# Turning attention weights by two rounded products with a unit matrix, at the head of each double step, instead of by plain fp32 transposes

## The reference

```
s = einsum('bqhd,bkhd->bhqk', q_i, k) * scale     # plus bias or decay, masked
p = softmax(s, axis=-1)
out = einsum('bhqk,bkhd->bqhd', p, v)
```

## Time and profile before

| | us |
|---|---|
| median of 3 runs (1578.36 to 1581.55) | 1580.87 |
| the profiled execution's own time | 1582.88 |
| its span, first to last instruction | 1581.0 |
| PE busy in it | 1538.2 (97%) |
| DVE busy | 1005.7 (64%) |
| ACT busy | 712.1 (45%) |
| POOL busy | 563.0 (36%) |

### The profile page before, as it was taken

How to read it: one execution, slowest core, us unless ns; L and a number is a source line. 1 busy time by engine, 2 the same in 40 slices (tenths; PEclk the granted TensorE clock), 3 DMA queues, 4 the chain that set the end, 5 groups by cost and what they waited for, 6 DMA issues and landing times.

```text
span 1581.0 us, 35399 instructions
## 1 busy us (share of the span) xinstructions
PE 1538.2 (97%) x15704; PEld 1414.6 (89%) x15704; DVE 1005.7 (64%) x1637; ACT 712.1 (45%) x1126; POOL 563.0 (36%) x452
## 2 busy tenths in 40 slices
PE   9999999999999999999999999999999999999998
PEld 8989987899978989987999989999998899999887
DVE  4364386878784445576777786766446777764356
ACT  4554534544445455435444444633332555433223
POOL 3745613000217745503000310734673006446640
PEclk9999999999999999999999999999999999999999
DMA  9433364787545423474676545453333354533332
GB/s 357 169 122 108 113 232 191 265 299 273 187 166 211 161 89 125 161 279 187 250 283 240 204 142 182 152 176 133 135 136 135 124 197 153 182 133 138 114 130 93
DMA packets 43944, 281.49 MB, mean 178 GB/s; under 512 B 5144, under 2 KB 5272, under 8 KB 14352
## 3 DMA queue, kind: packets, MB, share of 16 engines
q1 hardware_dynamic: 42192, 270.13, 47.4%
q0 software_dynamic: 1600, 9.10, 1.5%
HBM read 278.15 MB, written 1.06 MB: 177 GB/s over the span
## 4 chain that ended last, share of the span: by engine, by line
PE 78%; DVE 13%; ACT 3%; issue 3%; POOL 2%; DMA 0%; POOLq 0%; SPq 0%; ACTq 0%; DVEq 0%
PE ps L613 75%; DVE part0l L1453 3%; DVE part1l L1453 3%; PE ps L621 3%; ACT part0h L2523 1%; DVE rows L1890 1%; ACT part1h L2523 1%; DVE Pr L1887 1%; ACT gates L2520 1%; ACT Xh L2523 1%; DVE Xl L1468 1%; DVE small L1484 0%; DMA ring<-in_w 0%; DVE raw L2012 0%; DVE mgx L2144 0%
## 5 line engine op out<-in xcount | busy, mean ns | idle before, releaser
L2523 ACT ACTIVATE part1h<-ring 128x1024 fp32r<-128x1024 f32 (+1 forms) x216 | 215.8, 1047 | 226.0 <-PE ps L613 213.6
L2523 ACT ACTIVATE part0h<-ring 128x1024 fp32r<-128x1024 f32 (+1 forms) x216 | 213.0, 1035 | 209.6 <-PE ps L613 194.3
L613 PE MATMUL ps<-Xh,part1h 128*128 128x256 f32 x968 | 276.7, 286 | 7.5 <-DVE Xl L1468 2.4
L613 PE MATMUL ps<-Xh,part0h 128*128 128x256 f32 (+1 forms) x952 | 270.9, 285 | 3.4 <-DVE Xl L1468 1.3
L613 PE MATMUL ps<-Xl,part1h 128*128 128x256 f32 x968 | 271.1, 280 | 0.0
L613 PE MATMUL ps<-Xh,part1l 128*128 128x256 f32 x968 | 270.9, 280 | 0.0
L613 PE MATMUL ps<-Xl,part0h 128*128 128x256 f32 (+1 forms) x952 | 265.2, 279 | 0.0
L613 PE MATMUL ps<-Xh,part0l 128*128 128x256 f32 (+1 forms) x952 | 265.1, 278 | 0.0
L3020 POOL TENSOR_TENSOR part1l<-ring,part1h 128x512 fp32r<-128x512 f32 x144 | 185.3, 1317 | 102.5 <-ACT part1h L2523 102.3
L3020 POOL TENSOR_TENSOR part0l<-ring,part0h 128x512 fp32r<-128x512 f32 x144 | 185.3, 1318 | 101.8 <-ACT part0h L2523 101.7
L1453 DVE TENSOR_TENSOR part1l<-ring,part1h 128x1024 fp32r<-128x1024 f32 (+1 forms) x144 | 181.3, 1299 | 52.3 <-ACT part1h L2523 52.0
(11 more groups left out here) (446 smaller groups left out, 3260.4 us busy)
## 6 DMA issues: line engine op xcount, KB each, us to landing
ring<-in_w SPq DMA_DIRECT2D x211, 1024.0 KB, 4.9
hid<-in_ada SPq DMA_DIRECT2D x36, 512.0 KB, 6.3
hid<-in_w SPq DMA_DIRECT2D x6, 1024.0 KB, 11.1
rows<-in_lnrow POOLq DMA_DIRECT2D x6, 1024.0 KB, 9.9
fqk<-in_ada SPq DMA_DIRECT2D x6, 512.0 KB, 6.1
cq<-in_ada SPq DMA_DIRECT2D x6, 512.0 KB, 6.5
gates<-in_c SPq DMA_DIRECT2D x2, 1536.0 KB, 9.5
ring<-in_w SPq DMA_DIRECT2D x4, 512.0 KB, 5.6
```

The source lines that it names most:

```text
L613: return e.matmul(o, a, b, start=st, stop=sp)
L2523: return e.activation(o, a, ACT.Copy)
```

## The change

The transposes of the 12 pairs are replaced. ACT writes the rounded part of all four blocks of a pair (`Phigh`, fp32r), DVE the rest (`Plow = S2 - Phigh`, fp32r, in the place of `S2`). PE then makes two fp32r products with a rounded unit matrix for each block, high and low, summed in PSUM. `turn_two` does this for both units of a pair, and stands ahead of `weigh`. `Phigh` lies where `Sr2` and `Pr2` of kind `x` lie, so that the pT copies alternate between two `Pr` tiles and no longer three. In steps 0 to 3 DVE makes `Plow` ahead of its fill, from step 4 on behind it. Kind `x` keeps its transposes.

```
     def turn_weights(l, u):          # now for kind x alone
...
+    def turn_two(l, pair):
+
+        w.wait_ge(*at["unit_r"])
+        w.wait_ge(*at["low P", pair[0], l])
+        for y, u in enumerate(pair):
+            t, nt = ps.take(w, "pT", u, l), key_tiles(u)
+            for j in range(2):
+                for k in range(nt):
+                    o, keys = t[:, (j * nt + k) * 128:(j * nt + k + 1) * 128], slice(k * 128, (k + 1) * 128)
+                    mm(o, M.Ph[:, y, j, keys], M.unit_r, True, False)
+                    last = mm(o, M.Pl[:, y, j, keys], M.unit_r, False, True)
+            last.then_inc(*P("pT", u, l))
...
         for t in range(len(pairs) + 2):
+            if 1 <= t <= len(pairs):
+                turn_two(l, pairs[t - 1])
             if t >= 2:
                 for u in pairs[t - 2]:
                     weigh(l, u)
-            if 1 <= t <= len(pairs):
-                for u in pairs[t - 1]:
-                    turn_weights(l, u)
...
+    def low_weights(l, pair):        # DVE
+
+        u = pair[0]
+        nk = key_tiles(u) * 128
+        four = lambda t: t.rearrange("p y j k -> p (y j) k")[:, :, 0:nk]
+        w.wait_ge(*at["high P", u, l])
+        e.tensor_tensor(four(M.Pl), four(M.S2), four(f32(M.Ph)), ALU.subtract).then_inc(*V("low P", u, l))
...
-            between.fill()
+            if t >= 4:
+                between.fill()
+            if t < len(pairs):
+                low_weights(l, pairs[t])
+            if t < 4:
+                between.fill()
...
+    def high_weights(l, pair):       # ACT, behind the exponentials of pair t
+
+        u = pair[0]
+        nk = key_tiles(u) * 128
+        four = lambda t: t.rearrange("p y j k -> p (y j) k")[:, :, 0:nk]
+        old = scores_before(l, u)
+        if old:
+            w.wait_ge(*done["pT" if old[0][0] != "x" else "pv", old[0], old[1]])
+        w.wait_ge(*at["exp", pair[1], l])
+        copy(four(M.Ph), four(M.S2)).then_inc(*S("high P", u, l))
```

More of the change, by code:

```diff
@@ L326, in __init__ @@
         self.PcT = v(S("PcT", 256), g=2, n=128)
+        part = lambda stack, n: v(stack.enter_context(nc.sbuf_tensor(n, [128, 1024], F32R))[:, :], y=2, j=2, k=256)
+        with ExitStack() as early:
+            self.Pl, self.Ph = (part(early, n) for n in ("Plow", "Phigh"))
         self.S2 = v(S("S2", 1024), y=2, j=2, k=256)
         self.Sr = [self.S2[:, 0], self.S2[:, 1], v(S("Sr2", 512), j=2, k=256)]
-        self.Pr = [S(f"Pr{i}", 512) for i in range(3)]
+        self.Pr = [None, None, S("Pr2", 512)]
+        self.Pr[0:2] = [S(f"Pr{i}", 512) for i in range(2)]
+        self.unit_r = s1.enter_context(nc.sbuf_tensor("unit_r", [128, 128], F32R))[:, :]
         self.stat = stat = S("stat", 304)
@@ L435, with slot, slot_before @@
 UNITS = len(UNIT_NO)
-def slot(l, u):
-    return (UNITS * l + UNIT_NO[u]) % 3
-def score_slot(u):
+def slot(u):
     return (UNIT_NO[u] - UNIT_NO["x", 0, 0]) % 3 if u[0] == "x" else UNIT_NO[u] % 2
+def slot_before(l, u):
+    units = list(UNIT_NO)
+    n = UNIT_NO[u]
+    if u[0] == "x":
+        return (units[n - 3] if u[1:] == (1, 1) else ("m", 1, 1)), l
+    return (units[n - 2], l) if n > 1 else (("x", 1, 1), l - 1) if l else None
 def scores_before(l, u):
@@ L453, in scores_before @@
     return (units[n], l) if n > 0 else (("x", 1, 1), l - 1) if l else None
-def three_before(l, u):
-    n = UNITS * l + UNIT_NO[u] - 3
-    return None if n < 0 else (list(UNIT_NO)[n % UNITS], n // UNITS)
 def key_tiles(u):
@@ L765, in turn_weights @@
         w.wait_ge(*at["exp", u, l])
-        nt, S = key_tiles(u), M.Sr[score_slot(u)]
+        nt, S = key_tiles(u), M.Sr[slot(u)]
         for j in range(2):
@@ L775, in weigh @@
         w.wait_ge(*at["pT", u, l])
-        nt, pr, t = key_tiles(u), M.Pr[slot(l, u)], ps["o", u[0], u[1], l]
+        nt, pr, t = key_tiles(u), M.Pr[slot(u)], ps["o", u[0], u[1], l]
         for j in range(2):
@@ L1560, in turned_weights @@
         t = bank("pT", u, l)
-        old = three_before(l, u)
+        old = slot_before(l, u)
         if old:
@@ L1564, in turned_weights @@
         c = 2 * key_tiles(u) * 128
-        e.tensor_copy(M.Pr[slot(l, u)][:, 0:c], t[:, 0:c]).then_inc(*V("pT", u, l))
+        e.tensor_copy(M.Pr[slot(u)][:, 0:c], t[:, 0:c]).then_inc(*V("pT", u, l))
         ps.free(("pT", u, l), V.now())
@@ L1861, in mixer @@
         if l == 0:
+            after("cg")
+            e.tensor_copy(M.unit_r, M.ident).then_inc(*V("unit_r"))
             e.tensor_copy(M.hid[0:8, 1024:1536], bank("table")[0:8, :]).then_inc(*V("table"))
@@ L2598, in turned_weights @@
         c = 2 * key_tiles(u) * 128
-        copy(M.Pr[slot(l, u)][:, 0:c], t[:, 0:c]).then_inc(*S("pT", u, l))
+        copy(M.Pr[slot(u)][:, 0:c], t[:, 0:c]).then_inc(*S("pT", u, l))
         ps.free(("pT", u, l), S.now())
@@ L2608, in exponentials @@
         nk = key_tiles(u) * 128
-        s = M.Sr[score_slot(u)]
+        s = M.Sr[slot(u)]
         if u[0] == "x":
@@ L2626, in attention @@
                     turned_weights(l, u)
-            for u in pairs[t] if t < len(pairs) else ():
-                exponentials(l, u, pairs[t][0])
+            if t < len(pairs):
+                for u in pairs[t]:
+                    exponentials(l, u, pairs[t][0])
+                high_weights(l, pairs[t])
             between.fill()
```

## The result

The changed kernel takes 1605.01 us (median of 4 runs, 1602.32 to 1613.11) against 1579.61 us (4 runs, 1576.69 to 1581.55) for the one before: ratio 1.0171, 95% interval 1.0157 to 1.0186, slower. The forecast was 1609 us in a range of 1590 to 1622. The profiled execution took 1603.79 us, with a span of 1602.0.

What follows compares the result with a forecast made beforehand. PE, busy for 97% of the span, was taken to bound the kernel. Products at 13.8 us more and waits at 14 make 28 us on a median of 1581, so 1609 us, in a range of 1590 to 1622.

Steps and rivals of the forecast that it cites:

- Part 1: Turning on PE: 288 products at 0.113 us replace 144 transposes at 0.13 us, 13.8 us more.
- C: Product pace: loads overlap products more closely, 60 ns each, 1594 us with the waits; chance 0.12.
- D: Product pace: a short fp32r product costs as much as plain fp32, 0.224 us, giving 1641 us; chance 0.10.
- E: Product pace: products cost their columns alone, 53 ns, a gain of 3.3 us, 1577.6 us; chance 0.04.
- The 81 ns: Skill page's pace for loads and matmuls with 128 moving columns; turning would cost 4.6 us more instead of 13.8.
- Part 2: PE's waits at the head of five steps for late low parts: 14 us in both layers, bounds 0 and 24.
- rival B: Waits at step heads are hidden because ACT and DVE catch up: 1595 us; chance 0.08.
- step 11: Margin 0.65 us against 2.5 for the parts and 0.5 for the close: 2.35 us of waiting.
- step 9: Parts and later close exceed the 1.6 us margin by 2.0, plus 0.5 for DVE beside POOL: 2.5 us waiting.
- step 4: Margin 2.0 us against 2.5, and DVE's fill some 0.4 us later: 0.9 us of waiting.
- steps 0 and 5: Tight margin beside POOL in one, DVE's own long fill in the other: 1.2 us of waiting together, an estimate.
- Part 3: Two `Pr` tiles, unit matrix rounded at the start, ACT's copies delaying weight pieces up to 1 us: no cost.

Runs made afterwards that it cites:

- the run without waits: Changed kernel whose products read the rounded unit matrix as stationary side too, PE waiting for neither part, weights not turned: 1592.28 us, ratio 1.0084.
- the 256-column run: Changed kernel with the unit matrix twice as moving side, so each product moves 256 columns instead of 128: 1608.15 us, ratio 1.0184.
- the run with the waits alone: Changed kernel with one plain fp32 transpose of the high part per block instead of two products, both parts still made and waited for: 1587.84 us, ratio 1.0063.
- the second trace: Changed kernel again, nothing altered, run beside two later experiments and against the kernel before: 1609.24 us, ratio 1.0185.
- turning first: Kernel before with its transposes moved ahead of `weigh`, nothing else: 1577.83 us, ratio 0.9994.
- both: Changed kernel with all high products first, low ones behind their own wait, and `weigh` ahead of the turning: 1595.3 us, ratio 1.0105.

## Why the prediction was right, step by step

**Part 1, the price of the products: right.** Forecast 0.113 us for each and 13.8 us more; the trace has 0.111 us and 14.7 us, the run without waits 13.3. The small excess over 13.8 comes from the groups: a group of 16 ends 0.2 us behind its last start. The four-column rows were the right rows: they and the 256-column run bracket the case of 128 columns from both sides, 0.112, 0.111 and 0.120 us. Rivals C (60 ns) and D (224 ns) are out by the same number, and so is E, which needed under 65 ns. The one step that was taken on trust is that a rounded block loads at the pace of a plain one. The 81 ns of the Trainium skill's page "TensorE: Matmul & The Clock Gate", section "Back-to-back issue gap", don't hold for this stream of rounded products in the changed kernel, whose step was 0.111 us.

**Part 2, the waits: right in kind, in place but for step 5, and nearly in size.** Forecast 14 us, measured 10.8 and 12.0 in the two traces; rival B, under 4 us, is out, and the run with the waits alone costs 10.0 us. By step, in layer 0 of the first trace, with the 0.17 us in it:
- step 11, forecast 2.35: 2.58 measured, and nearly the same in both layers. The add of 1.58 us is in it; before had 1.20 at this place. With the add at 0.77 the wait was 1.80 + 0.17 = 1.97 in the run with the waits alone, so the forecast lies between the two cases, and how near it came is partly luck.
- step 9, forecast 2.0 + 0.5: 1.60 measured. This is the term that was mis-sized. Worked out from before's timing it was fair: the run with the waits alone, where steps keep before's length, has 2.16 + 0.17 = 2.33. The longer turning of the changed kernel moved DVE's add from beside POOL's stretch to its end, so the 0.94 us that the add can lose there were not lost. The 0.5 us that I had added for a subtraction beside POOL did not come either: it took 1.23 us and met POOL's next stretch only in its last 0.24 us.
- step 4, forecast 0.9: 0.61 measured.
- steps 0 and 5, forecast 1.2 together: 0.80 in layer 0 and 0.36 in layer 1, all of it step 0's, and 2.01 and 0.36 in the second trace, by the later weight piece. Step 5 had no wait. At step 0 the subtraction does lie beside POOL, and there it takes 1.24 us where the same form takes 0.69 clear of it:

```profile
45.29 1.24 DVE L1628 TENSOR_TENSOR Plow<-S,Phigh 128x512 fp32r<-128x512 f32 x1 [8.90 <-ACT Phigh L2553]
42.18 5.49 POOL L3063 TENSOR_TENSOR part0l<-ring,part0h 128x512 fp32r<-128x512 f32 x4 [1.70 <-ACT part0h L2553]
71.34 0.69 DVE L1628 TENSOR_TENSOR Plow<-S,Phigh 128x512 fp32r<-128x512 f32 x1 [2.44 <-ACT Phigh L2553]
```

So the contention that the forecast had put at step 9 fell on step 0, and most of the 0.63 us of that wait is this 0.55. What the forecast had no term for is the DMA.

**Part 3, the small edits at nothing: right.** No wait of PE for a bank, for weights or for the third buffer of turned weights is new. Turning ahead of weighing costs nothing without the two parts (0.9994), as I had put it: `weigh` was not work saved but cover given away.

**What the sum left out: the clock.** The changed kernel's eight executions lie at mean clocks of 0.989 to 0.996, those of before beside the second four at 0.995 to 0.998. The three of the changed kernel at 0.996 took 1602.3, 1603.8 and 1604.8 us; those at 0.989 to 0.991 took 1610.2 to 1613.1. That is some 8 us over a step of 0.006 and puts about 5 us on the changed kernel's average of 0.993 against 0.997, an estimate. So the forecast of 28 us, with the waits 2 to 3 us too high and the clock left out, came near the 25.4 and 29.5 of the two comparisons partly because two errors have opposite signs. The terms by themselves, 13.3 + 10.8 + 5 = 29, overshoot the mean of the two, 27.5, by less than 2, which is within what these medians scatter. By the ratios the two comparisons give 27.0 and 29.2. The clock's share is an estimate: no run held the work fixed and varied the clock.

## What to carry to other kernels

Where a block is loaded as the stationary side, count loads, not columns: splitting an operand in two nearly doubled the price of its turning here (0.222 us a block against 0.123 to 0.128), since one rounded product costs about what one transpose costs. When a change lengthens the chain between two visits of the busiest engine, take from the timeline how early the old input was there, and keep at that place something which doesn't depend on it: here 0.7 to 1.1 us of weighing and 0.9 us of high products gave back 10 of the 12 us or more that lay above the price of the products. And check which small contentions beside the chain meet it once the change has moved both: here the total stayed, but it went from one step to another.

## What was not expected of the hardware

- A product of 128 columns and one of 256 differ by 8% in pace (0.111 and 0.120 us), at full clock.
- A wait of 1 us or more of PE at the head of a step is followed, now and then, by a stretch at half clock. In the seven traces that have such waits there are 24 of them, and behind 7, within 2.2 us, the clock fell to its lower level; they are waits of 1.16 to 2.49 us. In the four traces without such a wait (before, turning first, no wait, both) no step of the two attentions shows one, but for a place at the start of layer 1's attention. PE waits 2.2 to 2.3 us for POOL's low part there in all eleven traces (before: 2.27 us, to 498.71), and in eight of them, before among them, the clock falls near the end of that wait. The two stretches of before near 1481 and 1539 us also stand behind waits of PE, of 1.42 and 1.94 us. Behind the 2.41-us wait of layer 0 a row of eight transposes took 1.97 us, where such a row takes about 1.1 at full clock; I put a stretch at 1.5 us, an estimate. Why the same wait brings it in layer 0 and not in layer 1 stays open, and no run varied it by itself.
- A DVE add of 512 columns took 1.77 us beside POOL's subtractions and 0.83 us nearly clear of them. DVE's subtraction of 512 columns took 1.24 us beside them and 0.69 clear of them. That of 1024 columns took at most 1.25 us in every trace, but in the changed kernel it never met them for more than 0.25 us, so nothing is shown of its case.
